# Forty tokens of the expert layer by fetched rows instead of thirty-two, and the second expert table in runs of 8 KB

## The reference

```python
def peer_ffn(h, w_query, sub_keys_1, sub_keys_2, expert_u, expert_v):
    # per token: 8 heads, two halves of 128 sub-keys each
    v1, i1 = lax.top_k(s1, 16)
    v2, i2 = lax.top_k(s2, 16)
    cand = v1[..., :, None] + v2[..., None, :]
    cand_idx = i1[..., :, None] * 128 + i2[..., None, :]
    best, pos = lax.top_k(cand.reshape(128, 8, 256), 16)
    idx = take_along_axis(cand_idx.reshape(...), pos)     # of 16384 experts
    g = softmax(best)
    act = gelu(einsum('td,thkd->thk', xc, expert_u[idx]))
    return einsum('thk,thkd->td', g * act, expert_v[idx])
```

## Time and profile before

| what | value |
|---|---|
| median of three runs | 1245.48 us (1244.26 to 1246.8) |
| the profiled execution's own time | 1244.98 us |
| its span, first to last instruction | 1243.7 us |
| TensorE busy / mean granted clock | 1210.4 us (97%) / 0.997 |
| weight load | 1026.3 us (83%) |
| VectorE busy | 1021.3 us (82%) |
| ScalarE busy | 719.8 us (58%) |
| GpSimd busy | 225.1 us (18%) |
| DMA, whole span | 266.45 MB, mean 214 GB/s |

### The profile page before, as it was taken

The page is one execution under the profiler, slowest core; times in us unless marked ns, Lnnn a source line. Parts: engine busy times, 40 slices in busy tenths (PEclk is TensorE's granted clock), DMA queues, the critical chain, the costliest instruction groups (busy, mean ns, idle before and its releaser), DMA issues.

```text
span 1243.7 us, 27066 instructions
## 1 busy us (share of the span) xinstructions
PE 1210.4 (97%) x11458; PEld 1026.3 (83%) x11458; DVE 1021.3 (82%) x1594; ACT 719.8 (58%) x1091; POOL 225.1 (18%) x202
## 2 busy tenths in 40 slices
PE   9989899999999999999999999999999999999996
PEld 6546785988644556549999999999999999999996
DVE  5767877999956766777899999899998888879985
ACT  5765334766646245746545468898875455545543
POOL 1323221445400000000113500000002221115320
PEclk9999999999999999999999999999999999999999
DMA  8521112756564422347537666555559999999981
GB/s 350 192 102 69 36 36 108 277 193 208 216 232 178 163 83 102 136 180 262 203 137 241 241 226 227 179 197 203 182 216 352 342 343 344 349 352 363 374 323 54
DMA packets 51353, 266.45 MB, mean 214 GB/s; under 512 B 5136, under 2 KB 5408, under 8 KB 32544
## 3 DMA queue, kind: packets, MB, share of 16 engines
q1 hardware_dynamic: 40192, 226.76, 50.6%
q0 software_dynamic: 10160, 35.96, 7.9%
q10 hardware_dynamic: 880, 1.99, 0.5%
HBM read 262.04 MB, written 2.10 MB: 212 GB/s over the span
## 4 chain that ended last, share of the span: by engine, by line
PE 83%; DVE 7%; ACT 4%; issue 3%; DMA 2%; POOL 0%; ACTq 0%; DVEq 0%; POOLq 0%
PE bank L725 24%; PE bank L728 24%; PE bank L731 24%; PE bank L1397 2%; DMA ring<-in_expert_v 1%; PE bank L805 1%; PE bank L1034 1%; PE bank L929 1%; PE bank L822 1%; PE bank L1345 1%; PE bank L876 1%; DVE HT L1636 1%; DVE arena L1529 1%; DVE arena L1636 1%; DVE ring L1889 0%
## 5 line engine op out<-in xcount | busy, mean ns | idle before, releaser
L725 PE MATMUL bank<-arena 128*128 128x256 f16 (+3 forms) x720 | 215.6, 306 | 1.5 <-DVE arena L1521 1.4
L731 PE MATMUL bank<-arena 128*128 128x256 f16 (+3 forms) x720 | 215.6, 306 | 0.0
L728 PE MATMUL bank<-arena 128*128 128x256 f16 (+3 forms) x720 | 215.6, 306 | 0.0
L1529 DVE SCALAR_TENSOR_TENSOR arena<-ring,arena 128x2048 f16<-128x2048 f32 (+1 forms) x59 | 133.8, 2272 | 31.0 <-ACT arena L2617 30.9
L725 PE MATMUL bank<-cst,arena 128*128 128x224 f16 (+2 forms) x544 | 133.3, 254 | 0.4 <-DVE arena L1529 0.4
L731 PE MATMUL bank<-cst,arena 128*128 128x224 f16 (+2 forms) x544 | 133.3, 254 | 0.0
L728 PE MATMUL bank<-cst,arena 128*128 128x224 f16 (+2 forms) x544 | 133.3, 254 | 0.0
L2617 ACT ACTIVATE arena<-ring 128x2048 f16<-128x2048 f32 (+1 forms) x59 | 111.1, 1892 | 28.9 <-PE bank L731 28.9
L2269 DVE SCALAR_TENSOR_TENSOR X<-ring,X 128x2048 f16<-128x2048 f32 x42 | 96.2, 2290 | 21.1 <-ACT X L3048 21.1
L3104 ACT CAST arena<-arena 128x448 f16<-128x448 f32 x64 | 36.1, 565 | 130.8 <-PE bank L731 130.8
L2269 DVE SCALAR_TENSOR_TENSOR ring<-ring 128x2048 f16<-128x2048 f32 x42 | 96.1, 2289 | 18.9 <-ACT ring L3048 18.9
(11 more groups left out here) (390 smaller groups left out, 3565.0 us busy)
## 6 DMA issues: line engine op xcount, KB each, us to landing
ring<-in_expert_u SPq DMA_DIRECT2D x64, 1024.0 KB, 4.8
ring<-in_expert_v SPq DMA_DIRECT2D x64, 1024.0 KB, 8.0
ring<-in_w_in_n SPq DMA_DIRECT2D x24, 1024.0 KB, 5.0
ring<-in_w_up_t SPq DMA_DIRECT2D x22, 1024.0 KB, 4.9
ring<-in_w_down_n SPq DMA_DIRECT2D x11, 1024.0 KB, 4.8
ring<-in_w_out_n SPq DMA_DIRECT2D x8, 1024.0 KB, 4.8
ring<-in_w_query_t SPq DMA_DIRECT2D x8, 1024.0 KB, 5.1
ring<-in_w_in_t SPq DMA_DIRECT2D x3, 1024.0 KB, 7.0
```

Of the source, the lines that this page charges most:

```text
L725: pe.matmul(out_, stat[0], mov[0], start=start, stop=False, skip_group_check=shared)
L728: pe.matmul(out_, stat[0], mov[1], start=False, stop=False, skip_group_check=shared)
L731: return pe.matmul(out_, stat[1], mov[0], start=False, stop=stop, skip_group_check=shared)
L1529: nv.scalar_tensor_tensor(out=lo, in0=ld.slot(i), scalar=W_UP, in1=hi, op0=ALU.mult, op1=ALU.subtract).then_inc(s["split_lo"], 1)
```

## The change

NG becomes 40: 216 tokens dense, 40 by rows. As 128 is no multiple of 40, the 40 tokens are two groups: tokens 8 to 39 lie on the partitions as before, 4 x 32, for steps 0 to 31; tokens 0 to 7 lie 16 times on 8 partitions each, and take steps 32 to 39. There are 40 + 40 fetches. Each group has its own activations and its own sums. All rows in come in the turns 64 to 93, one or two a turn (2, 1, 1 and again), all rows out in the turns 95 to 126 (2, 1, 1, 1). The second table is laid out in memory so that the two rows that a partition takes of a piece are neighbours, a run of 8 KB; the places of the fetched rows are computed for that order, in four more small operations, and both tables that are fetched from have it. At the end four products instead of two turn the row sums.

```diff
-NG = 32
+NG = 40
 NT = S - NG
-NK = 128 // NG
+ROW_GROUPS = [(8, 32), (0, 8)]
...
-ROWS_IN = [max(0, min(NG, n - 63)) for n in range(128)]
-ROWS_OUT = [max(0, min(NG, n - 95 + (n >= 110))) for n in range(128)]
-ROW_GELU = 95
+ROWS_IN = [max(0, min(NG, (4 * (n - 63) + 2) // 3)) for n in range(128)]
+ROWS_OUT = [max(0, min(NG, (5 * (n - 94) + 3) // 4)) for n in range(128)]
+ROW_GELU = 93
...
+def row_group(r):
+    return 0 if r < 32 else 1
+
+
+def row_buffer(n):
+    return n % 3
+
+
+def row_landed(n):
+    return 16 * sum(1 for i in range(n + 1) if row_buffer(i) == row_buffer(n))
+
+
+def row_before(n):
+    return max((i for i in range(n) if row_buffer(i) == row_buffer(n)), default=None)
...
-            self.src.append(d["expert_v"][256 * q:256 * (q + 1)].rearrange("(j p) n -> p j n", j=2))
+            self.src.append(d["expert_v"][256 * q:256 * (q + 1)].rearrange("(p j) n -> p j n", j=2))
...
             for hf in range(2):
-                pe.matmul(ps.tile("fin", 1, hf)[128 - NG:128, :], m.row_sel, m.row_sums[:, hf * 512:(hf + 1) * 512],
-                          start=True, stop=True)
+                for i in range(2):
+                    pe.matmul(ps.tile("fin", 1, hf)[64:128, :], m.row_sel[:, 64 * i:64 * i + 64],
+                              m.row_sums[i][:, hf * 512:(hf + 1) * 512], start=(i == 0), stop=(i == 1))
...
-            nv.scalar_tensor_tensor(out=m.places[0:NG, :], in0=m.selidx[0][0:NG, 1, :], scalar=128.0,
-                                    in1=m.selidx[0][0:NG, 0, :], op0=ALU.mult, op1=ALU.add)
+            first, second = (m.selidx[0][0:NG, i, :] for i in range(2))
+            pair = m.pair[0:NG, :]
+            c = step(nv.tensor_scalar(pair, second, 0.5, -0.25, ALU.mult, ALU.add))
+            after(c)
+            c = step(nv.tensor_scalar(pair, pair, ROUND, None, ALU.add))
+            after(c)
+            c = step(nv.tensor_scalar(pair, pair, -ROUND, None, ALU.add))
+            after(c)
+            c = step(nv.scalar_tensor_tensor(out=pair, in0=pair, scalar=254.0, in1=second, op0=ALU.mult, op1=ALU.add))
+            after(c)
+            nv.scalar_tensor_tensor(out=m.places[0:NG, :], in0=first, scalar=2.0, in1=pair, op0=ALU.mult, op1=ALU.add)
...
-        kk = r % 3
-        nv.wait_ge(s[f"fetched{kk}_landed"], 16 * (r // 3 + 1))
+        kk = row_buffer(r)
+        nv.wait_ge(s[f"fetched{kk}_landed"], row_landed(r))
         if r == 0:
-            nv.wait_ge(s["h_rows"], 4)
-        nv.tensor_tensor_reduce(out=m.fetched[kk], in0=m.fetched[kk], in1=m.h_rows, scale=1.0, scalar=0.0, op0=ALU.mult,
+            nv.wait_ge(s["h_rows"], 8)
+        nv.tensor_tensor_reduce(out=m.fetched[kk], in0=m.fetched[kk], in1=m.h_rows[row_group(r)], scale=1.0, scalar=0.0, op0=ALU.mult,
                                 op1=ALU.add, accum_out=m.row_dots[:, r:r + 1]).then_inc(s["rows_used"], 1)
...
     def row_out(r):
 
         n = NG + r
-        kk = n % 3
-        nv.wait_ge(s[f"fetched{kk}_landed"], 16 * (n // 3 + 1))
+        kk = row_buffer(n)
+        sums = m.row_sums[row_group(r)]
+        nv.wait_ge(s[f"fetched{kk}_landed"], row_landed(n))
+        nv.wait_ge(s["rows_used"], n)
         if r == 0:
             nv.wait_ge(s["row_weights"], 1)
-            nv.wait_ge(s["rows_used"], NG)
-            ins = nv.tensor_scalar(m.row_sums, m.fetched[kk], m.row_dots[:, 0:1], None, ALU.mult)
+        if r == 0 or row_group(r) != row_group(r - 1):
+            ins = nv.tensor_scalar(sums, m.fetched[kk], m.row_dots[:, r:r + 1], None, ALU.mult)
         else:
-            nv.wait_ge(s["rows_used"], n)
-            ins = nv.scalar_tensor_tensor(out=m.row_sums, in0=m.fetched[kk], scalar=m.row_dots[:, r:r + 1],
-                                          in1=m.row_sums, op0=ALU.mult, op1=ALU.add)
+            ins = nv.scalar_tensor_tensor(out=sums, in0=m.fetched[kk], scalar=m.row_dots[:, r:r + 1],
+                                          in1=sums, op0=ALU.mult, op1=ALU.add)
         ins.then_inc(s["rows_used"], 1)
...
+    def place_tokens(group):
+        first, count = ROW_GROUPS[group]
+        for i in range(128 // count):
+            ng.dma_start(m.h_rows[group][i * count:(i + 1) * count, :],
+                         m.xs[3][first:first + count, 0, :]).then_inc(s["rows_placed"], 16)
+
+    def place_rows(group):
+        first, count = ROW_GROUPS[group]
+        per = 128 // (128 // count)
+        c0 = 32 * group
+        for i in range(128 // count):
+            rows, at = slice(i * count, (i + 1) * count), slice(i * per, (i + 1) * per)
+            ng.dma_start(m.row_at[rows, c0:c0 + per], m.places[first:first + count, at]).then_inc(s["rows_placed"], 16)
+            ng.dma_start(m.row_gate[rows, c0:c0 + per],
+                         m.slot_gate[0].rearrange("p h k -> p (h k)")[first:first + count, at]
+                         ).then_inc(s["rows_placed"], 16)
+
+    place_tokens(0)
+    place_tokens(1)
     ng.dma_start(m.fetched[0], k.d["ffn_g"]).then_inc(s["row_gain_landed"], 16)
     choose(0)
     ng.wait_ge(s["slots_named"], 1)
-    for i in range(NK):
-        rows, at = slice(i * NG, (i + 1) * NG), slice(i * NG, (i + 1) * NG)
-        ng.dma_start(m.row_at[rows, :], m.places[0:NG, at]).then_inc(s["rows_placed"], 16)
-        ng.dma_start(m.row_gate[rows, :],
-                     m.slot_gate[0].rearrange("p h k -> p (h k)")[0:NG, at]).then_inc(s["rows_placed"], 16)
+    place_rows(0)
     choose(1)
-    ng.wait_ge(s["rows_placed"], 16 * 3 * NK)
+    place_rows(1)
...
     for n in range(2 * NG):
         if n == 0:
-            ng.wait_ge(s["h_rows"], 4)
+            ng.wait_ge(s["h_rows"], 8)
         if n == 1:
             ng.wait_ge(*ps.full("u", [q for i, q in enumerate(SPLIT) if k.halves(i) == 2][-1]))
-        if n >= 3:
-            ng.wait_ge(s["rows_used"], n - 2)
+        if row_before(n) is not None:
+            ng.wait_ge(s["rows_used"], row_before(n) + 1)
+        kk = row_buffer(n)
         ng.indirect_dma_start(
-            out=m.fetched[n % 3], out_offset=None, in_=k.d["expert_rows" if n < NG else "expert_v"],
+            out=m.fetched[kk], out_offset=None, in_=k.d["expert_rows" if n < NG else "expert_v"],
             in_offset=bass.IndirectOffsetOnAxis(ap=m.row_at[:, n % NG:n % NG + 1], axis=0),
-        ).then_inc(s[f"fetched{n % 3}_landed"], 16)
+        ).then_inc(s[f"fetched{kk}_landed"], 16)
...
-    ur, ev = (x[n][0].reshape(128, 128, 1024).transpose(1, 0, 2).reshape(16384, 1024)
```

More of the change, by code:

```diff
@@ L154 @@
 NCOLS = _o
-ROWS = [("foxo", 64), ("gdno", 64), ("hgo", 64), ("glao", 64), ("alog", 4), ("dtb", 4), ("foxb", 4), ("glab", 128)]
+ROW_CONSTS = [("foxo", 64), ("gdno", 64), ("hgo", 64), ("glao", 64), ("alog", 4), ("dtb", 4), ("foxb", 4), ("glab", 128)]
 ROW_AT = {}
 _o = 0
-for _n, _w in ROWS:
+for _n, _w in ROW_CONSTS:
     ROW_AT[_n] = (_o, _w)
@@ L450, in memory @@
     g = Arena(t, 128 * NT, 32768)
-    m.h_rows = g.take(1024)
+    m.h_rows = [g.take(1024) for _ in range(2)]
     m.row_sums = m.h_rows
@@ L455, in memory @@
     m.row_at = g.take(NG).bitcast(U32)
-    m.row_gate, m.row_dots, m.row_sel = (g.take(NG) for _ in range(3))
+    m.row_gate, m.row_dots = (g.take(NG) for _ in range(2))
+    m.row_sel = m.rows[:, 256:384]
+    early = Arena(t, 12800, 14336)
     a = Arena(t, 16384, 128 * NT)
@@ L460, in memory @@
     m.s2 = [a.take(128) for _ in range(2)]
[L461 to L465, removed]
+    m.top = [x_.take(16, 16) for x_ in (early, a)]
+    m.idx = [x_.take(16, 16) for x_ in (early, a)]
+    m.idf = [x_.take(16, 16) for x_ in (early, a)]
+    m.best = [x_.take(8, 16) for x_ in (early, a)]
+    m.pos = [x_.take(8, 16) for x_ in (early, a)]
     m.cand = m.qq[:, 0:8, :]
@@ L475, in memory @@
     m.places = a.take(128).bitcast(U32)
+    m.pair = a.take(128)
     m.eq = [f16(m.qq[:, 8 + 4 * i:12 + 4 * i, :].rearrange("p a n -> p (a n)"), 64, 32) for i in range(2)]
@@ L2501, in vector_program @@
     weigh_late(63)
-    nv.tensor_reduce(m.row_sel, ident.rearrange("p (k f) -> p f k", k=NK), AX.X, ALU.add).then_inc(s["row_sel_one"], 1)
+    nv.memset(m.row_sel, 0.0).then_inc(s["row_sel_one"], 1)
     nv.wait_ge(s["row_sel_one"], 1)
+    for i, (_, count) in enumerate(ROW_GROUPS):
+        at = 64 * i + (32 if i == 0 else 24)
+        nv.tensor_reduce(m.row_sel[:, at:at + count], ident.rearrange("p (k f) -> p f k", f=count), AX.X,
+                         ALU.add).then_inc(s["row_sel_one"], 1)
+    nv.wait_ge(s["row_sel_one"], 3)
     nv.tensor_scalar(m.row_sel, m.row_sel, W_UP, None, ALU.mult).then_inc(s["row_sel"], 1)
@@ L3068, in gelu @@
         if q == min(LATE, 14336 // (2 * NT)):
-            na.wait_ge(s["rows_placed"], 16 * 3 * NK)
+            na.wait_ge(s["rows_placed"], 16 * 3 * (128 // 32 + 128 // 8))
         src = ps.tile("u", q)[:, :].rearrange("p (j n) -> p j n", j=2)
@@ L3345, in choose @@
             ins.then_inc(s["candidates"], 1)
-    for i in range(NK):
```

(33 more changed lines are left out.)

## The result

The changed kernel takes 1277.05 us (median of 4 runs, 1276.11 to 1279.37), the kernel before on the same chip 1246.14 us: a ratio of 1.0251, 95% interval 1.0235 to 1.0266. It is slower by 31 us; forecast was 1247 us, range 1225 to 1262. The profiled execution has a span of 1276.0 us (before 1243.7).

A forecast was written before the change was run, and what follows sets the result against it. TensorE was taken as the bound, VectorE and DMA close behind. First half -11.1, rows in +6.9, rows out 0, pieces without rows -0.3, start +1.0, read back +2.0, late landings +1.5, end +1.9: +1.9 us, 1247 us, range 1225 to 1262.

The forecast's parts named there:

- TensorE's columns, 92.5 ns a matmul: Dense matmuls: 216 columns instead of 224 take 92.5 ns, 3.3 ns less; -10.2 us in either half.
- First half, cover for -11.1 us: First half of dense work: VectorE, busy 267.5 of 289 us, has room to follow TensorE, so all -11.1 us are gained.
- the first half does not follow: Rival, first half: VectorE or ScalarE becomes its bound, half of 11.1 us lost, 1252 us; chance 0.05.
- Three buffers at the new rate: Second half: row fetches through three buffers set the pace, 4.83 us a piece in rows in (+6.9 us), 4.60 in rows out.
- Rows out: 0: Second half, second table: with landings of 9.0 us the pace stays at 4.60 us a piece, so 0 us.
- The 8 KB layout, taken as 0: Second table's transfers: 8 KB packets cost the same per byte as 4 KB ones, 0 us, within 4% of transfer time.
- Start +1.0: Start of the second half: waiting for row 1, now due near 940.7 us, adds +1.0 us.
- late landings +1.5: Second half: landings near 9 us that occur now and then anyway add +1.5 us.
- read back +2.0: Second half: reading back residual and gain (1.6 MB) stalls the buffers without spare time, +2.0 us (bounds 0 and 6).
- End +1.9: Kernel end: four 512-column products instead of two turn the row sums, on the path, +1.9 us.
- The row fetches slow down further: Rival, second half: landings take 10 us, giving 5.17 and 4.85 us a piece, +18.6 us, 1264 us; chance 0.18.
- TensorE keeps its pace: Rival, second half: others follow TensorE at 4.44 us a piece, -18.4 us, 1227 us; chance 0.27, wholly or partly.

The follow-up runs named there:

- Experiment 8: Changed kernel with five row buffers and, from the third gate group on, low halves of the one-hot gates multiplied for a quarter only: 1231.55 us, 0.9891.
- experiment 1: Changed kernel with the 8 KB layout taken back (second table in its old order, 4 KB runs): 1270.25 us, 1.0197 of the kernel before.
- experiment 2: Changed kernel with five buffers for fetched rows instead of three: 1238.31 us, 0.9946 of the kernel before.
- experiment 10: Changed kernel with four row buffers instead of three: 1236.53 us, 0.9932 of the kernel before.
- experiment 6: Kernel before with only the new timetable of row turns (2, 1, 1 and 2, 1, 1, 1), still 32 rows and 224 columns: 1261.96 us, 1.0133.
- experiment 5: Kernel before with the 8 KB layout of the second table alone: 1245.06 us, 0.9999.
- experiment 7: Changed kernel with five row buffers and the second table in 4 KB runs: 1239.11 us, 0.994 of the kernel before.
- experiment 3: Changed kernel, three buffers, with VectorE's row operation put ahead of the low halves of the answers: 1261.33 us, 1.0131 of the kernel before.

## Why the prediction was wrong

- **TensorE's columns, 92.5 ns a matmul:** right. Experiment 8 shows that the first half gives 10.5 of the forecast 11.1 us where VectorE doesn't bind.
- **First half, cover for -11.1 us:** wrong, -5.4. The forecast set VectorE's 267.5 us against 289 us for the whole stretch. The gates come in bursts, and in a late turn with one VectorE needs 5.69 us where TensorE now needs 5.37. The rival "the first half does not follow" had the right mechanism and, at half of 11.1, nearly the right price; its chance of 0.05 was too low. Cost: 5.7 us.
- **Three buffers at the new rate:** the step that failed by the most, in size and not in kind. The loop was the one described: late issues, a wait for the DMA ahead of the row operations, and TensorE behind it. L, the time from issue to landing, was taken as 9.0. Over all fetches it was 9.3 and 10.1, and over those that VectorE waited for 10.3 and 11.3. The first pair, put into the forecast's own formulas, gives (5.5 + 9.32)/3 = 4.94 and (9.4 + 10.12)/4 = 4.88 us a turn; the second gives 5.28 and 5.17, where 5.29 and 5.12 were measured. So the formulas held, and the L in them has to be that of the late-issued fetches on the loop; a mean over all takes in those with a quick issue, which have time to spare. The match isn't perfect: the same reading of experiment 1 (9.9 and 10.1 us) gives 5.13 and 4.88, where 5.24 and 4.89 were measured, so up to 0.1 us a turn can be the scatter of landings or the second chain, through the row behind the double turn, which the forecast left out. More buffers (experiments 2, 10) remove the loop, and the rate alone (experiment 6) makes it.
- **"Rows out: 0":** wrong by +15.6 us. L was thought to be equal in both; the landings waited for were 1 us longer in rows out. 0.8 us of the landings there is the layout (experiment 1).
- **The 8 KB layout, taken as 0:** right beside slack (experiments 5, 7), wrong in the loop (7 us, experiment 1). The forecast's bound of 1.5 us in L held with three buffers, where the value was 0 for rows in and 0.8 for rows out; with five it was 1 to 2 us (experiment 7).
- **Start +1.0, late landings +1.5, read back +2.0:** not to be told apart in the ring, whose pace contains them. With more buffers the read back shows as TensorE stalls of 1.71 us at 1112 us (five) and 2.79 us at 1111 us (four).
- **End +1.9:** +3.6. The row sums took 5.24 us and not 3.76, after 1.31 us of waiting (1.10 in the earlier trace rows):

```profile
1252.85 5.24 PE L1476 MATMUL bank<-arena,rows 128*64 128x512 f32 x8 [1.31 <-DVE arena L2490]
```

- **Together,** against the forecast: first half +5.7, rows in +13.8 (0.46 x 30), rows out +15.6 (0.52 x 30), end +1.7, the three edge terms, contained in the pace, -4.5, and a rest of about -2 that was not traced: +30, from 1247 to 1277 us.
- **The rivals.** "The row fetches slow down further" was the true one: it gave 5.17 and 4.85 us a turn at L = 10, and 1264 us. Its counterweight, that a slower pace would shorten L, is refuted: at 334 GB/s, less than the 344 before, L did not fall, because the issue stays late (2.75 us); whether the pairs of fetches add to it is not shown. "TensorE keeps its pace" is nearly what four buffers give (4.55 us a turn; 1236.5 us, of which 5.7 us are the first half and some 3 us the read back).

What stays open: why the rest of a landing, behind its issue, is 7.0 to 7.7 us at 334 GB/s and was 6.2 in rows in before at 344. The new timetable, with its pairs of fetches, goes with it (6.8 in experiment 6); the layout is a part in rows out alone (experiment 1). Nothing here separates pairs from rate.

## What to carry to other kernels

Before a rate is raised, go round each loop of buffers: (work in the loop + issue + landing) / buffers, with the landings of those fetches that the loop waits for, late issues included, and not with a mean over all; where that is near the pace, buy one more buffer first. Here one buffer of 4 KB a partition turned 2.5% slower into 0.7% faster. And don't set averages of busy time against the bound: the turn with the most work decides, and its length is in the timeline. A cost measured in a state with slack (the layout, the late issue) says little of the same cost in a state without.

## What the runs showed of the hardware

- The granted clock fell behind stalls. TensorE stood still for 2.74 us up to 1023.17 us in the changed kernel, and between 1024 and 1028 us the granted clock was 0.57, near the lower of its two levels (1.2 of 2.4 GHz): 28 matmuls where the stretch 1016 to 1020 has 46. Mean over 940 to 1216 us: 0.97. It did not set the time there: VectorE's turn at 1027.0 us took 3.86 us without a wait meanwhile, and TensorE waits behind it.
- The core moved 374 GB/s over 276 us with its DMA engines busy for 0.96 of the time (0.97 in experiment 7, with the old packets), against 344 before at 0.95. The busy share of the DMA engines thus isn't a measure of how much more they can carry.
- A fetch whose issue is ahead of VectorE's long operation by 0.16 us is hardly delayed (1.06 us instead of 0.94, 43 times in experiment 3); one that starts 0.35 us into it takes 2.75 us (55 times in the changed kernel).
